# The opening of a three-branch layer on one core: the norm's weights transposed first, and the work behind them in another order

## The reference, cut to what matters

```python
def rmsnorm(x, w, eps=NORM_EPS):
    x32 = x.astype(jnp.float32)
    y = x32 * lax.rsqrt(jnp.mean(x32 * x32, axis=-1, keepdims=True) + eps)
    return (y * w.astype(jnp.float32)).astype(x.dtype)
...
h = rmsnorm(x, norm_w[l])
p = h @ w_in[l]
```

## Time and profile before

| | |
|---|---|
| median of 3 runs | 1115.96 us (1115.7 to 1116.47) |
| the profiled execution's own time | 1117.01 us |
| its span | 1115.3 us |
| mean granted clock of TensorE | 0.996 |
| TensorE busy | 1100.5 us (99%) |
| VectorE, ScalarE, GpSimd busy | 807.8, 610.7, 42.5 us |

### The profile page before, as it was taken

One profiled execution on the slowest core, in us unless ns is written; L12 is line 12 of the kernel. 1 busy time (PEld: TensorE's weight loads), 2 busy tenths in 40 slices (PEclk: granted clock), 3 DMA queues, 4 the chain that ended last, 5 costly groups with the idle time before them and its releaser, 6 DMA issues.

```text
span 1115.3 us, 22920 instructions
## 1 busy us (share of the span) xinstructions
PE 1100.5 (99%) x8006; PEld 918.8 (82%) x8006; DVE 807.8 (72%) x1257; ACT 610.7 (55%) x934; POOL 42.5 (4%) x68
## 2 busy tenths in 40 slices
PE   7999999999999999999999999999999999999997
PEld 5888888888888888888888888888888888888885
DVE  6888889798897988889888858445555555556564
ACT  6666575665756657576475645445344544435443
POOL 2000000000000000000000120000000000000000
PEclk8999999999999999999999999999999999999999
DMA  7766656556475655656556565666666576667663
GB/s 200 206 162 181 171 141 171 157 160 167 129 189 148 180 152 141 183 144 176 143 164 176 153 189 156 222 207 189 191 191 196 158 226 200 195 179 270 212 192 109
DMA packets 254556, 197.24 MB, mean 177 GB/s; under 512 B 23111, under 2 KB 206640, under 8 KB 254128
## 3 DMA queue, kind: packets, MB, share of 16 engines
q1 hardware_dynamic: 251748, 195.81, 60.6%
q10 hardware_dynamic: 2764, 0.85, 0.3%
HBM read 193.71 MB, written 2.11 MB: 176 GB/s over the span
## 4 chain that ended last, share of the span: by engine, by line
PE 98%; DVE 1%; ACT 1%; ACTq 0%; issue 0%
PE ps L1372 31%; PE ps L1375 15%; PE ps L1473 12%; PE ps L1475 12%; PE ps L1474 12%; PE ps L1761 3%; PE ps L1762 3%; PE ps L1760 3%; PE ps L1507 1%; PE ps L1685 1%; PE ps L1546 0%; PE ps L1402 0%; PE ps L1645 0%; PE ps L1709 0%; PE ps L1554 0%; PE ps L1582 0%
## 5 line engine op out<-in xcount | busy, mean ns | idle before, releaser
L853 DVE TENSOR_TENSOR wlo<-raw,whi 128x1024 fp32r<-128x1024 f32 x352 | 434.3, 1247 | 218.4 <-ACT whi L455 216.6
L1372 PE MATMUL ps<-hx,whi 128*128 128x512 f32 x1424 | 516.2, 405 | 1.4 <-DVE hx L884 1.3
L455 ACT ACTIVATE whi<-raw 128x1024 fp32r<-128x1024 f32 (+1 forms) x356 | 370.3, 1051 | 252.8 <-PE ps L1475 182.4
L1375 PE MATMUL ps<-hx,wlo 128*128 128x256 f32 x1424 | 399.6, 281 | 0.0
L1372 PEld LDWEIGHTS ps<-hx,whi 128*128 128x128 f32 x1424 | 268.0, 188 | 69.1 <-issue 6.9
L1375 PEld LDWEIGHTS ps<-hx,wlo 128*128 128x128 f32 x1424 | 269.8, 189 | 1.1 <-DVE lots L893 0.5
L1473 PE MATMUL ps<-whi,hx 128*128 128x512 f32 x384 | 150.4, 392 | 0.0
L1475 PE MATMUL ps<-whi,hx 128*128 128x512 f32 x384 | 149.6, 390 | 0.0
L1474 PE MATMUL ps<-wlo,hx 128*128 128x512 f32 x384 | 149.5, 389 | 0.0
L1475 PEld LDWEIGHTS ps<-whi,hx 128*128 128x128 f32 x384 | 72.1, 188 | 15.0
L1473 PEld LDWEIGHTS ps<-whi,hx 128*128 128x128 f32 x384 | 72.1, 188 | 14.9 <-issue 0.2
(11 more groups left out here) (285 smaller groups left out, 1048.4 us busy)
## 6 DMA issues: line engine op xcount, KB each, us to landing
raw<-in_w_in SPq DMA_DIRECT2D x548, 256.0 KB, 3.2
raw<-in_w_branch SPq DMA_DIRECT2D x96, 256.0 KB, 3.7
raw<-in_w_out SPq DMA_DIRECT2D x64, 256.0 KB, 3.7
o<-in_x SPq DMA_DIRECT2D x4, 512.0 KB, 5.6
o<-in_x SPq DMA_DIRECT2D x2, 1024.0 KB, 8.7
acb<-acs_rows SPq DMA_DIRECT2D x7, 256.0 KB, 3.4
out_y<-lots SPq DMA_DIRECT2D x5, 256.0 KB, 2.5
lots<-in_final_norm_w SPq DMA_DIRECT2D x1, 1024.0 KB, 11.5
```

The costliest lines, as they stand in the source:

```text
L455: sc.activation(whi[:, slot, :, 0:width], raw[:, slot, :, 0:width], ACT.Copy).then_inc(hi_done, 1)
L853: tt(wlo[:, slot, :, :], raw[:, slot, :, :], whi[:, slot, :, :].bitcast(F32), ALU.subtract).then_inc(lo_done, 1)
L1372: mm(ps[:, bank, :], whi[:, slot, k, wcol], hx[:, kt].rearrange("p a t -> p (a t)"), start=first, stop=False, skip_group_check=True)
L1375: return mm(ps[:, bank, 0:T], wlo[:, slot, k, wcol], hhi[:, kt, :], start=False, stop=last, skip_group_check=True)
```

## The change

The input norm's weights get a load and a transpose of their own. norm_w is loaded once more, first on ScalarE's queue, into `nrow` (16 rows of 128), and TensorE transposes that alone after the b = 0 tiles; ScalarE copies its 16 columns into `prm`. All thirteen vectors still come as before, now behind chunk 1 on SP's queue (not behind chunk 0), and are brought to partitions by two products with the identity behind strip 0's last step; ScalarE copies them after the sixteenth high part of h, and VectorE's `omm` and `halfb` wait for that copy. TensorE makes three zero products behind the norm weights' transpose. On VectorE the reciprocal and the first 256 columns of b = 1 come after four of the nine copies and mask operations; 512 more columns are scaled behind the first low part of h; the last 1280 columns of b = 1 are scaled by GpSimd. The other five mask operations come behind the sixteenth low part. TensorE transposes two tiles of b = 1 ahead of strip 0 and four behind its first step. Some semaphores are merged (`x_rt` with `f_act`, `x_rs` with `f_rs`, `dt_ae` into `dt_e`).

```diff
 # SP
-            strip(0, (RANKS, DT0), (P, 16), first=True, quarters=range(0, 1))
+            strip(0, (RANKS, DT0), (P, 16), first=True, quarters=range(0, 2))
             for r0, src in rows[6:]:
                 sp.dma_start(prow[r0 % P:r0 % P + src.shape[0], r0 // P, :], src).then_inc(prm_in, 16)
-            strip(0, (RANKS, DT0), (P, 16), first=True, quarters=range(1, 4))
+            strip(0, (RANKS, DT0), (P, 16), first=True, quarters=range(2, 4))
...
 # GpSimd, behind the constants
+            pool.wait_ge(s["row_rs"], 2)
+            rest = xtok[:, 1, 6 * P:D]
+            gp.tensor_scalar(rest, rest, rowst[:, 5:6], None, ALU.mult).then_inc(s["x_np"], 1)
...
 # ScalarE
+            act.dma_start(nrow, norm_w.rearrange(by_tile, c=P)).then_inc(s["norm_in"], 16)
             for r0, src in rows[:6]:
...
             split_hi(0, 0, 1, P + 16, first=True)
             act.wait_ge(s["prm_t"], 1)
-            sc.activation(prm[:, 0:ROWS0], ps[:, 3, 0:ROWS0], ACT.Copy)
-            sc.activation(prm[:, P:P + ROWS1], ps[:, 3, P:P + ROWS1], ACT.Copy).then_inc(s["prm_ok"], 1)
+            sc.activation(prm[:, NW:NW + KT], ps[:, 3, 0:KT], ACT.Copy).then_inc(s["prm_ok"], 1)
             act.wait_ge(s["prm_ok"], 1)
...
                 if k in (3, 7, 11):
                     split_hi(1 + k // 4, 1 + k // 4, 1, P + 16, first=True)
+            act.wait_ge(s["prm_t"], 2)
+            sc.activation(prm[:, 0:ROWS0], ps[:, 6, 0:ROWS0], ACT.Copy)
+            sc.activation(prm[:, P:P + ROWS1], ps[:, 6, P:P + ROWS1], ACT.Copy).then_inc(s["prm_ok"], 1)
             act.wait_ge(s["prm_d"], 1)
...
 # VectorE
+            row_factor(0)
+            scale_rows(0, 0, 2 * P)
+            scale_rows(0, 2 * P, 4 * P)
+            scale_rows(0, 6 * P, 10 * P)
             dve.wait_ge(s["const_m"], 1)
...
             tt(mask64[:, 3, :], mask4[:, 1, own], mask4[:, 1, other], ALU.add)
+            row_factor(1)
+            scale_rows(1, 0, 2 * P)
...
+            split_lo_ranks(0)
+            dve.wait_ge(s["prm_ok"], 1)
+            for k in range(KT):
+                dve.wait_ge(s["h_hi"], k + 1)
+                stt(hlo[:, k, :], ...).then_inc(s["h_lo"], 1)
+                if k == 0:
+                    scale_rows(1, 2 * P, 4 * P)
+                if k in (3, 7, 11):
+                    split_lo_ranks(1 + k // 4)
+            v.memset(steps[:, :, 0:1], 1.0)
...
+            dve.wait_ge(s["prm_ok"], 2)
             ts(omm[:], prm[:, MU:MU + 33], -1.0, 1.0, ALU.mult, ALU.add)
             ts(halfb[:], prm[:, W0:W0 + 16], 0.5, None, ALU.mult).then_inc(s["prm_d"], 1)
...
 # TensorE
-            pe.wait_ge(prm_in, 13 * 16)
-            tr(ps[:, 3, 0:ROWS0], prow[0:ROWS0, 0, :], ident[0:ROWS0, 0:ROWS0])
-            tr(ps[:, 3, P:P + ROWS1], prow[0:ROWS1, 1, :], ident[0:ROWS1, 0:ROWS1]).then_inc(s["prm_t"], 1)
-            for k in range(6):
+            pe.wait_ge(s["norm_in"], 16)
+            tr(ps[:, 3, 0:KT], nrow, ident[0:KT, 0:KT]).then_inc(s["prm_t"], 1)
+            for n in range(3):
+                mm(ps[:, 2, :], zeros[:, 0:P], zeros[:, 0:512], start=True, stop=True)
+            for k in range(2):
                 scaled_rows(1, k)
                 x_tile(k, 1).then_inc(s["x_tr"], 1)
...
+                        if kt == 0:
+                            for n in range(2, 6):
+                                scaled_rows(1, n)
+                                x_tile(n, 1).then_inc(s["x_tr"], 1)
                         if kt + 6 < KT:
                             scaled_rows(1, kt + 6)
                             x_tile(kt + 6, 0)
                             x_tile(kt + 6, 1).then_inc(s["x_tr"], 1)
+                    if q == 3:
+                        pe.wait_ge(prm_in, 13 * 16)
+                        mm(ps[:, 6, 0:ROWS0], prow[0:ROWS0, 0, :], ident[0:ROWS0, 0:ROWS0], start=True, stop=True)
+                        mm(ps[:, 6, P:P + ROWS1], prow[0:ROWS1, 1, :], ident[0:ROWS1, 0:ROWS1], start=True, stop=True
+                           ).then_inc(s["prm_t"], 1)
```

More of the change, by code:

```diff
@@ L112, in build_program @@
         lshift = lot(15)
+        nrow = lots[0:16, 31, 0:P]
         prow = lot(16).rearrange("p (a c) -> p a c", a=2)
@@ L224, in build_program @@
         low_out = sem("low_out")
-        names = """zeros_z f_sum z_ok pad_z const_z const_b const_m const_o prm_t prm_ok prm_d x_sq x_rt x_rs x_n x_tr h_hi h_lo ranks_sh lr_ok
-            bc_s bc_th bc_ok sc_mm scm_ok dt_lo dt_v dt_e dt_l dt_ae acs_ok
+        names = """zeros_z f_sum z_ok pad_z const_z const_b const_m const_o norm_in prm_t prm_ok prm_d x_sq row_rt row_rs x_n x_np x_tr h_hi h_lo ranks_sh lr_ok
+            bc_s bc_th bc_ok sc_mm scm_ok dt_lo dt_v dt_e dt_l  acs_ok
             dt_tr dat_ok shifted qq_ok halved tap_ok lora_mm tanh_wa sig_wa cum exps kk_ok kk_sq kk_mm kk_max kk_rt kk_rin
@@ L232, in build_program @@
             acs_st acb_in seg_ok seg_e seg_g yb_mm ob_d ob_ok sq_ok gn_mm gn_rt gn_r gn_ok osp_hi osp_lo gy_ok
-            mg_ok mt m_hi m_lo out_mm out_ok f_sq f_act f_rs f_ok f_hi stored"""
+            mg_ok mt m_hi m_lo out_mm out_ok f_sq   f_ok f_hi stored"""
         s = {n: sem(n) for n in names.split()}
@@ L449, in _ @@
                 sc.activation(rowst[:, 2 + b:3 + b], rowst[:, 9 + 2 * b:10 + 2 * b], ACT.Sqrt, scale=1.0 / D,
-                              bias=rowst[:, b:b + 1]).then_inc(s["x_rt"], 1)
+                              bias=rowst[:, b:b + 1]).then_inc(s["row_rt"], 1)
             def split_hi(c, slot, use, width=CW, first=False):
@@ L563, in _ @@
                     sc.activation(dts[:, 2, :], dts[:, 1, :], ACT.Exp, scale=-1.0).then_inc(s["dt_e"], 1)
-                    sc.activation(dtc[:, 2:3], dtc[:, 1:2], ACT.Exp).then_inc(s["dt_ae"], 1)
+                    sc.activation(dtc[:, 2:3], dtc[:, 1:2], ACT.Exp).then_inc(s["dt_e"], 1)
                     act.wait_ge(s["dt_v"], 2)
@@ L798, in row_root @@
                 sc.activation(rowst[:, 2 + b:3 + b], rowst[:, b:b + 1], ACT.Sqrt, scale=1.0 / D, bias=eps3[:, 0:1]
-                              ).then_inc(s["f_act"], 1)
-                act.wait_ge(s["f_rs"], b + 1)
+                              ).then_inc(s["row_rt"], 1)
+                act.wait_ge(s["row_rs"], b + 3)
             row_root(0)
@@ L823, in _, with row_factor, scale_rows @@
             v.memset(scx[:], 0.0).then_inc(s["zeros_z"], 1)
[L825 to L834, removed]
+            def row_factor(b):
+                dve.wait_ge(s["row_rt"], b + 1)
+                v.reciprocal(rowst[:, 4 + b:5 + b], rowst[:, 2 + b:3 + b]).then_inc(s["row_rs"], 1)
+                dve.wait_ge(s["row_rs"], b + 1)
+            def scale_rows(b, at, w):
+                part = xtok[:, b, at:at + w]
+                ts(part, part, rowst[:, 4 + b:5 + b], None, ALU.mult).then_inc(s["x_n"], 1)
+            row_factor(0)
+            scale_rows(0, 0, 2 * P)
+            scale_rows(0, 2 * P, 4 * P)
+            scale_rows(0, 6 * P, 10 * P)
             dve.wait_ge(s["const_m"], 1)
@@ L879, in _ @@
             dve.wait_ge(s["prm_ok"], 1)
-            v.memset(steps[:, :, 0:1], 1.0)
             for k in range(KT):
@@ L885, in _ @@
                     ALU.mult, ALU.subtract).then_inc(s["h_lo"], 1)
+                if k == 0:
+                    scale_rows(1, 2 * P, 4 * P)
                 if k in (3, 7, 11):
                     split_lo_ranks(1 + k // 4)
+            v.memset(steps[:, :, 0:1], 1.0)
+            tt(mask64[:, 0:2, :], mask4[:, 0:2, own], mask4[:, 0:2, other], ALU.add).then_inc(s["const_o"], 1)
+            dve.wait_ge(s["const_o"], 1)
+            tt(mask64[:, 2, :], mask64[:, 0, :], m16c[:], ALU.subtract)
+            stt(centre[:], head1[:], -1.0 / 64, ident[:], ALU.mult, ALU.add)
+            v.tensor_reduce(id32[:], ident[:].rearrange("p (a n) -> p n a", a=4), AX.X, ALU.add)
+            v.tensor_reduce(par[:].rearrange("p h u -> p (h u)"), m16b.rearrange("p (a n) -> p n a", a=4), AX.X, ALU.add
+                            ).then_inc(s["const_o"], 1)
+            dve.wait_ge(s["prm_ok"], 2)
             ts(omm[:], prm[:, MU:MU + 33], -1.0, 1.0, ALU.mult, ALU.add)
@@ L976, in _ @@
                     dve.wait_ge(s["dt_v"], 7)
-                    dve.wait_ge(s["dt_ae"], 1)
+                    dve.wait_ge(s["dt_e"], 2)
                     ts(dts[:, 3, :], dts[:, 5, :], dtc[:, 2:3], -1.0, ALU.mult, ALU.mult).then_inc(s["dt_v"], 1)
@@ L1307, in row_scale @@
                     v.tensor_reduce(rowst[:, b:b + 1], rowst[:, 8 + 4 * b:12 + 4 * b], AX.X, ALU.add).then_inc(s["f_sum"], 1)
-                    dve.wait_ge(s["f_act"], b + 1)
-                    v.reciprocal(rowst[:, 4 + b:5 + b], rowst[:, 2 + b:3 + b]).then_inc(s["f_rs"], 1)
-                    dve.wait_ge(s["f_rs"], b + 1)
+                    dve.wait_ge(s["row_rt"], b + 3)
+                    v.reciprocal(rowst[:, 4 + b:5 + b], rowst[:, 2 + b:3 + b]).then_inc(s["row_rs"], 1)
+                    dve.wait_ge(s["row_rs"], b + 3)
```

(4 more changed lines are left out.)

## The result

The changed kernel took 1121.36 us (median of 6 runs, 1120.5 to 1122.78), the kernel before 1116.05 beside it (6 runs, 1115.45 to 1116.47): ratio 1.005, 95% interval 1.0041 to 1.006, or 5.3 us slower. The forecast was 3.4 us slower, 1119.4, with a range to 1122.3. The profiled execution took 1121.2 us, its span is 1119.5; that is 4.2 us over the span of before.

A forecast was written before the change was run, and what follows sets the result against it. TensorE, with 98% of the chain of waits, was taken to bound the kernel. Opening -1.7, wait before strip 1 +3.4 and clock +1.7 gave +3.4 us: 1119.4 us, range 1115.0 to 1122.3 (forecast's own range 1118.2 to 1121).

The forecast's parts named there:

- The hand-over: From strip 0's last product to strip 1's start: 3.95 us in place of 0.57, a loss of 3.4 us.
- The clock behind it: After strip 1's start: the granted clock falls behind TensorE's 3.3 us gap, losing 1.7 us, at most 3.4.
- The first rival: TensorE stalls before strip 1 but the clock holds: +1.7 us, 1117.7; chance 0.25.
- The opening: Up to step 4 of strip 0: step 4 starts at 18.8, not 20.48, a gain of 1.7 us.
- the lock: Before step 0: VectorE's two-input split stands while GpSimd scales, so it runs from 13.5 to 14.35.
- a sign of being wrong: Strip 1 starting within 1.5 us of strip 0's last product, or step 4 after 20.
- its signs of being right: TensorE idle 3 us before strip 1, ScalarE idle, first split late or long, step 4 at 18 to 19.5, clock 0.50.
- nearer to the memset: 1.7: GpSimd's scaling of 1280 columns in the opening takes 1.7 us, between bounds of 1.3 and 3.0.
- All at the upper level: Strip 0's steps up to step 4 run at the upper clock, 0.80 us a step, not 1.48.
- second rival: Opening gains only 0 to 0.4 us, by a clock fall or GpSimd needing 3 us: +5.1, 1121.1; chance 0.15.
- The zero products: Three in TensorE's gap in the opening, at most 0.85 us each, from 10.05 to 12.6.
- The third rival: GpSimd's scaling costs VectorE nothing, opening gains 2.5 us, clock holds: +0.7 us, 1116.7; chance 0.13.

The follow-up runs named there:

- e1: Changed kernel with the parameters' copy and VectorE's two factors moved behind the splits of chunks 4 to 6: 1116.98 us, ratio 1.0008 to the kernel before.
- e2: Changed kernel with GpSimd's 1280 columns scaled by VectorE, right behind its split of chunk 0: 1119.37 us, ratio 1.0028 to the kernel before.
- e5: Changed kernel with six zero products of 256 columns behind the parameters' products, filling TensorE's gap before strip 1: 1119.64 us, ratio 1.0035 to the kernel before.
- e6: Changed kernel with GpSimd's scaling made to wait for VectorE's split of chunk 0: 1120.81 us, ratio 1.0043 to the kernel before.
- e4: The kernel of e3 without the three zero products in the opening: 1114.95 us, ratio 0.9994 to the kernel before.
- e3: Changed kernel with the edits of e1 and e2 together: 1113.73 us, ratio 0.9983 to the kernel before.
- e7: The kernel of e3 with two zero products, not three, and VectorE's 1280 columns in two pieces, 256 and 1024: 1113.07 us, ratio 0.9977 to the kernel before.
- e8: Changed kernel once more, unaltered, for one profile: 1121.58 us, span 1119.9.

## Why the prediction was right, and where it was off

**The hand-over: right, term for term.** Forecast 3.95 us in place of 0.57, measured 3.97: the products start 0.23 behind the last one (29.37), the copies end at 30.41 (1.04 later, forecast 1.0), the factors start at 30.44, and from there to strip 1 it is 2.67 (forecast 2.66). e1 takes it out and 4.7 us with it.

**The clock behind it: right, the size near in part by luck.** 1.7 forecast, 1.47 measured; the stretch lasted 3.41 us, half of the 6.84 that gave the bound, and TensorE worked in all of it. In e2 the clock fell 1.1 us before the end of the same gap and stayed low for 6.83 us, which cost 2.7 us (8.30 from strip 1's start to pair 16; 5.63 in e1, which has the same pace and no fall there). e5 speaks for the gap as the cause. The first rival, in which the clock holds, fell.

**The opening: the lock (VectorE's split stands while GpSimd works) right, the gain wrong in sign.** Forecast a gain of 1.7 us, measured a loss of 0.5: step 4 started at 21.00, not at 18.8, and lies behind the 20 that the prediction itself named as a sign of being wrong (of its signs of being right, all came but step 4 at 18 to 19.5). Two of its terms failed. The first is the length of GpSimd's scaling, "nearer to the memset: 1.7". GpSimd needed 3.67 us beside VectorE and 3.52 in e6, 2.75 ns a column, above the bound of 3.0 that I took from a sum of two tensors (2.35 ns a column). I thought that a product by one number per row could not cost more than a sum of two tensors; no row said so. The lock did the rest as forecast: split and remainder ended at 15.2 instead of 14.35, step 0 started at 15.75 instead of 14.9. With this term alone step 4 starts at 19.53, as in e5, whose opening is the changed kernel's without the fall: 0.7 us late. The second is "All at the upper level": the clock fell at 16.25, and that took the other 1.5 us (19.53 to 21.00).

Both conditions of the second rival came true ("GpSimd needs 3 us", and the clock falls after the wait before step 0), but its "gain 0 to 0.4" reckoned with one of them at a time. That its +5.1 is near the measured +5.3 is in part luck: its terms add up to 5.5 in the ledger, of which 1.3 came back unforeseen, and the two profiled executions differ by 4.2. The measured 1121.36 lies just outside the forecast's own range of 1118.2 to 1121. The rival should have had more than 0.15, since the bound for an operation that no row shows was only the dearest row at hand.

By the Trainium skill's "SBUF — State Buffer", section Who interferes with whom, a GpSimd instruction that reads SBUF and a VectorE one that reads two tensors from SBUF, or that takes both port pairs as a scaling can, exclude each other, and the second stands for the whole of the first. The trace agrees where VectorE is second (3.39 and 2.86 us); no run here shows GpSimd held that long. By the Trainium skill's "GPSIMD Engine Reference", section 3.1, which puts a loop that its ports bound at about one cycle per element, the estimate for the scaling was 1.2 us; the measured 3.52 decides against it.

**The zero products: right.** They ran from 10.05 to 12.73 (forecast 12.6) at the upper level, and by e4 they are worth 2.2 us at strip 1's start in the kernel of e3 (1.2 in the medians). The third rival, no cost on VectorE, fell with the 3.39.

**Not foreseen:** 1.3 us that came back behind pair 16. 0.85 of it is the pace of pairs 16 to 144 (below); the other 0.4 is no more than two executions of the changed kernel differ by from pair 144 on (0.6).

## What to carry to other kernels

A wait that is put into an engine's list holds back everything behind it: ask not who reads the data late enough, but which instruction of the next stage stands behind the copy (here the split of chunk 4, for 3.4 us and a fall of the clock). Work given to an idle GpSimd is not free where VectorE's next instruction reads two tensors from SBUF or scales one: here that instruction stood until GpSimd was through, so the price was near GpSimd's full length, 3.5 us for what VectorE did in 0.88. A gap of 3 us in TensorE's work cost the gap and, through the clock, another 1.5 to 2.7 us behind it (the changed kernel, e2); products by zero went with a clock that held, both in the opening (e3 against e4) and at the hand-over (e5), and are worth a try where a gap can't be closed.

## What the runs showed of the hardware that was not expected

- GpSimd's product of 1280 columns by one value per row took 3.52 us with no VectorE instruction under way at its start (e6), VectorE's 0.88 (e2); GpSimd's sum of two tensors of 1024 columns takes 2.40.
- A pair of products takes 353 ns, between pairs 16 and 144 (strips 1 to 5), in some programs (before, e3, e4, e5) and 347 in others (the changed kernel, e1, e2, e6, e7) at a granted clock of 1.00 in all of them. Both of the programs profiled twice kept theirs. It is worth 0.85 us over these 128 pairs, for the kernels with 347; what decides it is open.
- With the same wait before step 0 the clock fell in three executions of four, at 16.25 (the changed kernel), 16.95 (e1) and 17.05 (e8). Whether that is what spreads the changed kernel's runs over 2.3 us (1120.5 to 1122.78) is not shown: the 23 runs of before beside e1 spread over 2.2.
